# Decoder step on one core: a shared bias table row, projections between spatial-gating steps, and a pooled-row store moved ahead of the table loads

## What is computed

```python
qa,ka,va,fa,ub,vb,qc,kc,vc,pd = split(x @ w_in)
o_a = fox_attention(qa, ka, va, cumsum(log_sigmoid(fa + b)))     # A, per-head forget gate
u, v = gelu(ub), layer_norm(gelu(vb), g, b)                      # B, gating unit in chunks of 128
o_b = u * (tril(w_spatial) @ v + b_spatial)
o_c = dilated_attention(qc, kc, vc, t5_bias)                     # C, bias from a 32-bucket table
o_d = (trailing_mean(pd) - pd) @ w_pool * pool_scale             # D
x = LN(ALPHA*x + (sum_n sigmoid(x @ w_gate_n) * (o_n @ w_branch_n)) @ w_out)
x = LN(ALPHA*x + moe(x))                                         # 16 experts, top 2
```

## Time and profile before

| | us |
|---|---|
| median of 3 runs | 1513.4 |
| lowest, highest | 1512.94, 1513.81 |
| profiled execution | 1514.06 |
| its span, first to last instruction | 1512.1 |

### The profile page before, as it was taken

How to read it: one execution, slowest core, us unless ns; L and a number is a source line. 1 busy time by engine, 2 the same in 40 slices (tenths; PEclk the granted TensorE clock), 3 DMA queues, 4 the chain that set the end, 5 groups by cost and what they waited for, 6 DMA issues and landing times.

```text
span 1512.1 us, 20414 instructions
## 1 busy us (share of the span) xinstructions
PE 1371.3 (91%) x7682; PEld 1094.0 (72%) x7682; DVE 779.9 (52%) x1336; ACT 480.7 (32%) x788; POOL 322.8 (21%) x233
## 2 busy tenths in 40 slices
PE   6989989979788999999999999999928999999970
PEld 5665565756555799999999999778826666677640
DVE  3465474542245422344444344464775677777746
ACT  3311145421136311111111111221125556555636
POOL 0258910353453000000000000000245112223220
PEclk9989999999979999999999999999959999999995
DMA  7347620355601121321321431422387998887645
GB/s 226 117 134 263 212 98 1 107 182 169 221 17 32 64 81 63 108 80 64 107 80 65 144 126 66 150 78 79 122 311 280 379 310 312 297 310 254 202 153 226
DMA packets 75197, 237.72 MB, mean 157 GB/s; under 512 B 17029, under 2 KB 27476, under 8 KB 61422
## 3 DMA queue, kind: packets, MB, share of 16 engines
q1 hardware_dynamic: 48630, 160.73, 29.7%
q0 software_dynamic: 17792, 59.20, 13.2%
q10 hardware_dynamic: 8704, 16.84, 3.2%
HBM read 213.49 MB, written 65.74 MB: 185 GB/s over the span
## 4 chain that ended last, share of the span: by engine, by line
PE 83%; DMA 5%; DVE 4%; ACT 3%; issue 2%; POOL 2%; SPq 0%; DVEq 0%; POOLq 0%
PE ps L481 16%; PE ps L483 16%; PE ps L482 16%; PE ps L620 7%; PE ps L1257 6%; PE ps L1229 5%; PE ps L1253 2%; PE ps L1354 2%; PE ps L1254 2%; PE ps L1397 2%; PE ps L1255 2%; DMA b<-in_state_k 2%; PE ps L545 1%; DMA out_pool_p<-b 1%; DMA tmp_yd<-b,b 1%
## 5 line engine op out<-in xcount | busy, mean ns | idle before, releaser
L481 PE MATMUL ps<-b,b 128*128 128x344 f32 (+1 forms) x1360 | 469.1, 345 | 5.4 <-DVE b L841 2.7
L483 PE MATMUL ps<-b,b 128*128 128x344 f32 (+1 forms) x1360 | 465.1, 342 | 0.0
L482 PE MATMUL ps<-b,b 128*128 128x344 f32 (+1 forms) x1360 | 464.9, 342 | 0.0
L481 PEld LDWEIGHTS ps<-b,b 128*128 128x128 f32 x1360 | 254.9, 187 | 24.5 <-issue 3.5
L483 PEld LDWEIGHTS ps<-b,b 128*128 128x128 f32 x1360 | 254.6, 187 | 19.2 <-issue 0.9
L482 PEld LDWEIGHTS ps<-b,b 128*128 128x128 f32 x1360 | 254.6, 187 | 17.2 <-issue 0.9
L1012 DVE TENSOR_TENSOR b<-b,b 128x2048 fp32r<-128x2048 f32 x64 | 146.6, 2291 | 66.2 <-ACT b L704 60.0
L649 ACT ACTIVATE b<-ps,b 128x344 f32<-128x344 f32 x96 | 52.7, 549 | 380.2 <-PE ps L483 380.2
L1083 POOL DMA_INDIRECT tmp_xs<-b,b x36 | 43.1, 1198 | 593.1 <-issue 572.4
L1229 PE MATMUL ps<-b,b 128*128 128x128 f32 (+1 forms) x782 | 119.1, 285 | 39.2 <-DMA b<-tmp_xs 18.4
L1229 PEld LDWEIGHTS ps<-b,b 128*128 128x128 f32 (+1 forms) x782 | 93.0, 145 | 83.4 <-issue 35.6
(11 more groups left out here) (290 smaller groups left out, 1556.0 us busy)
## 6 DMA issues: line engine op xcount, KB each, us to landing
b<-in_w SPq DMA_DIRECT2D x96, 1024.0 KB
b<-in_w_merge SPq DMA_DIRECT2D x32, 640.5 KB, 4.3
tmp_xs<-b ACTq DMA_DIRECT2D x32, 514.0 KB, 4.3
b<-tmp_xs SPq DMA_DIRECT2D x32, 514.0 KB
b<-in_w_in SPq DMA_DIRECT2D x8, 1024.0 KB, 8.8
b<-in_xT SPq DMA_DIRECT2D x4, 1024.0 KB, 11.9
b<-in_w_out SPq DMA_DIRECT2D x4, 1024.0 KB, 8.2
b<-in_x SPq DMA_DIRECT2D x8, 512.0 KB, 4.0
```

The source lines that it names most:

```text
L481: mm(out, hi, mhi, start=start, stop=False)
L482: mm(out, hi, mlo, start=False, stop=False)
L483: return mm(out, lo, mhi, start=False, stop=stop)
```

## The change

1. **Bias table.** 12 matmuls with 32 output rows each, the four heads in four groups of 32 rows of the same banks (5, 6 and 7), in pieces of 512, 512 and 128 columns. ACT copies three pieces into one row block `tb_row`, and the store repeats each row four times. The PE never waits for ACT in it. DVE no longer waits for the store (`tb_out`), POOL waits for `tb_src` instead.
2. **Gating unit.** The subtraction of the mean and the gain are done per tile during the `uv` stage, the rest in one unlinked operation a tile. The `vfa` tiles, now in the order 2 to 7, 0, 1, stand between the sample tiles, the spatial matmuls and the transposes. The sample row's product comes first on DVE.
3. **Splits of the `vpd` weights** stand before the last `qkc` eviction on ACT, one weight chunk per finished chunk of the last `qkc` tile (`pk`), and earlier on DVE.
4. **Late stores.** `pool_p` is stored as soon as the last `vpd` tile is evicted, ahead of the table loads.
5. **First merged tile.** DVE makes high and low part itself: chunks 0 to 6 before the last weight's product, chunk 7 behind it. PE waits for chunk 7 only at its last k.

POOL's order of gathers and dilated keys is as before.

```diff
--- before.py
+++ after.py
...
+VFA_ORDER = (2, 3, 4, 5, 6, 7, 0, 1)
+
+PROJECTED = ([("uv", t) for t in TILE_ORDER] + [("vfa", NT)] + [("vfa", t) for t in VFA_ORDER[:2]] + [("qka", NT)]
+             + [("vfa", t) for t in VFA_ORDER[2:]]
...
-        tb_src = at(OT + 4608, [P, 4, TBW])
+        tb_row = at(PSB, [P, TBW])
...
-                pe.wait_ge(S("mlo"), s + 1)
+                pe.wait_ge(S("mlo"), s + 2 if s else 1)
+                if s == 0 and n == 0:
+                    pe.wait_ge(S("sgd"), 95)
                 if n == 0:
                     pe.wait_ge(S("wo0s"), 8)
                 for k in range(KD):
+                    if s == 0 and n == 0 and k == KD - 1:
+                        pe.wait_ge(S("mlo"), 2)
...
-            merged_high(0)
...
-            for u in range(2):
-                merge_weight(KD // 2 - 1, 3, u, u == 1)
-                split_out_weights(KD - 2 + u, KD - 1 + u)
+
+            def first_tile(chunks):
+                t = WORDER[0]
+                r = rows(t)
+                hi, m = mring[:, 0, chunks, 0:r], mT[:, chunks, t * P:t * P + r]
+                link(dve.tensor_copy(hi, m))
+                dve.tensor_tensor(mL[:, chunks, t * P:t * P + r], m, hi.bitcast(F32), ALU.subtract).then_inc(S("mlo"), 1)
+
+            merge_weight(KD // 2 - 1, 3, 0, False)
+            split_out_weights(KD - 2, KD - 1)
+            split_out_weights(KD - 1, KD)
+            first_tile(slice(0, KD - 1))
+            merge_weight(KD // 2 - 1, 3, 1, True)
             dve.sem_inc(S("merged"), 1)
+            first_tile(slice(KD - 1, KD))
...
-                dve.wait_ge(S("mhi"), s + 1)
+                dve.wait_ge(S("mhi"), s)
                 m = mT[:, :, t * P:t * P + r]
                 dve.tensor_tensor(mL[:, :, t * P:t * P + r], m, mring[:, s % 3, :, 0:r].bitcast(F32), ALU.subtract).then_inc(S("mlo"), 1)
 
-            merged_low(0)
...
-            sp.wait_ge(S("tb_src"), 12)
-            sp.dma_start(a["tb_dram"].rearrange("h (p u) -> p h u", p=P), tb_src[:]).then_inc(S("tb_out"), 16)
+            sp.wait_ge(S("tb_src"), 1)
+            sp.dma_start(a["tb_dram"].rearrange("h (r i u) -> (h r) i u", i=H, u=TBW),
+                         tb_row[:].rearrange("r (o u) -> r o u", o=1).to_broadcast([P, H, TBW])).then_inc(S("tb_out"), 16)
...
-            sp.wait_ge(S("proj"), 45)
+            sp.wait_ge(S("evicted"), pj_index("vpd", NT - 1) + 1)
+            sp.dma_start(a["pool_p"], vp[P - 15:P, NT - 1, W:2 * W]).then_inc(S("out_pool"), 16)
             for h in range(H):
                 src = a["tb_dram"][h, P - 1:P - 1 + P * (TBW - 1)].rearrange("(p u) -> p u", u=TBW - 1)[:, 0:SEQ]
                 sp.dma_start(tb[:, h, :], src).then_inc(S("tb_in"), 16)
-            sp.wait_ge(S("evicted"), pj_index("vpd", NT - 1) + 1)
             sp.dma_start(a["v_c_p"].rearrange("(t p) w -> p t w", p=P), vp[:, :, 0:W]).then_inc(S("out_vc"), 16)
-            sp.dma_start(a["pool_p"], vp[P - 15:P, NT - 1, W:2 * W]).then_inc(S("out_pool"), 16)
...
+                        if chunk == "qkc" and t == NT - 1 and k < KD - 1:
+                            m.then_inc(S("pk"), 1)
...
-            for h in range(H):
-                for q in range(3):
-                    n = h * 3 + q
-                    if n >= 2:
-                        pe.wait_ge(S("tb_src"), n - 1)
-                    mm(ps[:, 6 + n % 2, 0:384], t5[:, h:h + 1].to_broadcast([NBUCK + 1, P]), oh_rev[:, q * 384:(q + 1) * 384],
-                       start=True, stop=True).then_inc(S("tb_mm"), 1)
-            pe.wait_ge(S("tb_src"), 12)
+            for n, (lo, hi) in enumerate(TB_PARTS):
+                for h in range(H):
+                    m = mm(ps[32 * h:32 * h + 32, 5 + n, 0:hi - lo], t5[:, h:h + 1].to_broadcast([NBUCK + 1, 32]), oh_rev[:, lo:hi],
+                           start=True, stop=True)
+            m.then_inc(S("tb_mm"), 1)
             for i in range(4):
-                m = mm(ps[:, 6, i * H:(i + 1) * H], oh_dec[:, i, :], t5[:], start=True, stop=True)
+                m = mm(ps[:, 4, i * H:(i + 1) * H], oh_dec[:, i, :], t5[:], start=True, stop=True)
             m.then_inc(S("tb_mm"), 1)
 
-            project("vfa", NT)
-            project("qka", NT)
-            pe.wait_ge(S("wsp_m"), 4)
-            pe.wait_ge(S("v_done"), 1)
-            for g in range(4):
-                if g >= 2:
-                    pe.wait_ge(S("ob"), g - 1)
-                elif g == 0:
-                    pe.wait_ge(S("tb_src"), 13)
+            def spatial(g):
+                if g == 0:
+                    pe.wait_ge(S("wsp_m"), 4)
+                    pe.wait_ge(S("v_done"), 1)
+                    pe.wait_ge(S("tb_src"), 1)
+                elif g >= 2:
+                    pe.wait_ge(S("ob"), g)
                 mm(ps[:, 6 + g % 2, :].rearrange("p (t c) -> p t c", t=NT), wsp[:, g, :],
                    uv[:, 0:NT, W + 64 * g:W + 64 * g + 64], start=True, stop=True).then_inc(S("band_mm"), 1)
-            pe.wait_ge(S("ob"), 5)
-            for t in range(NT + 1):
-                if t >= 2:
-                    pe.wait_ge(S("obT"), t - 1)
-                r = rows(t)
-                for f in range(2):
-                    m = tr(ps[:, 4 + t % 2, f * P:f * P + r], uv[0:r, t, f * P:(f + 1) * P], r)
-                m.then_inc(S("ob_tr"), 1)
+
+            def ob_transposes(*tiles):
+                for t in tiles:
+                    if t == 0:
+                        pe.wait_ge(S("ob"), 5)
+                        pe.wait_ge(S("tb_src"), 2)
+                    if t >= 2:
+                        pe.wait_ge(S("obT"), t - 1)
+                    r = rows(t)
+                    for f in range(2):
+                        m = tr(ps[:, 4 + t % 2, f * P:f * P + r], uv[0:r, t, f * P:(f + 1) * P], r)
+                    m.then_inc(S("ob_tr"), 1)
+
+            project("vfa", NT)
+            project("vfa", VFA_ORDER[0])
+            project("vfa", VFA_ORDER[1])
+            project("qka", NT)
+            spatial(0)
+            spatial(1)
+            project("vfa", VFA_ORDER[2])
+            spatial(2)
+            spatial(3)
+            project("vfa", VFA_ORDER[3])
+            ob_transposes(0, 1)
+            project("vfa", VFA_ORDER[4])
+            ob_transposes(2, 3)
+            project("vfa", VFA_ORDER[5])
+            ob_transposes(4, 5)
+            project("vfa", VFA_ORDER[6])
+            ob_transposes(6, 7, 8)
+            project("vfa", VFA_ORDER[7])
...
-            for t in TILE_ORDER[1:]:
-                project("vfa", t)
...
-                if chunk == "vpd":
-                    act.wait_ge(S("proj"), pj_index("qkc", NT - 1) + 1)
                 for k in range(KD):
+                    if chunk == "vpd" and k < KD - 1:
+                        act.wait_ge(S("pk"), k + 1)
+                    elif chunk == "vpd":
+                        act.wait_ge(S("proj"), pj_index("qkc", NT - 1) + 1)
...
-            for n in range(12):
-                h, q = n // 3, n % 3
-                act.wait_ge(S("tb_mm"), n + 1)
-                act.copy(tb_src[:, h, q * 384:(q + 1) * 384], ps[:, 6 + n % 2, 0:384]).then_inc(S("tb_src"), 1)
-            act.wait_ge(S("tb_mm"), 13)
-            act.copy(bC[:].rearrange("p s h -> p (s h)"), ps[:, 6, 0:16]).then_inc(S("tb_src"), 1)
+            act.wait_ge(S("tb_mm"), 1)
+            for n, (lo, hi) in enumerate(TB_PARTS):
+                m = act.copy(tb_row[:, lo:hi], ps[:, 5 + n, 0:hi - lo])
+            m.then_inc(S("tb_src"), 1)
+            act.wait_ge(S("tb_mm"), 2)
+            act.copy(bC[:].rearrange("p s h -> p (s h)"), ps[:, 4, 0:16]).then_inc(S("tb_src"), 1)
             evict("vfa", NT)
+            evict("vfa", VFA_ORDER[0])
+            evict("vfa", VFA_ORDER[1])
             evict("qka", NT)
-            for t in TILE_ORDER[1:]:
+            for t in VFA_ORDER[2:]:
...
+                else:
+                    w_high("vpd")
                 evict("qkc", i - 1)
+                if i == 8:
+                    x_high("vpd", 1)
                 values_ready(i)
-            w_high("vpd")
-            x_high("vpd", 1)
...
+                v = uv[0:r, t, W:2 * W]
+                dve.scalar_tensor_tensor(v, v, mv[0:r, t, 0:1], gbB[0:r, 0, :], ALU.subtract, ALU.mult)
                 if 3 <= i <= 6:
                     x_low("uv", i + 1)
             dve.tensor_scalar(rs2[:], mv[:, :, 1], EPS, None, ALU.add).then_inc(S("var"), 1)
             dve.wait_ge(S("sd"), 1)
             link(dve.reciprocal(rs[:], rs[:]))
-            for t in range(NT + 1):
+            for t in range(NT, -1, -1):
                 r = rows(t)
                 v = uv[0:r, t, W:2 * W]
-                link(dve.tensor_scalar(v, v, mv[0:r, t, 0:1], rs[0:r, t:t + 1], ALU.subtract, ALU.mult))
-                link(dve.tensor_tensor(v, v, gbB[0:r, 0, :], ALU.mult))
-                link(dve.tensor_tensor(v, v, gbB[0:r, 1, :], ALU.add))
```

(22 more changed lines are left out.)

7 lines of the change are left out of this document (4 added, 3 removed).

## The result

| | us |
|---|---|
| before, median | 1513.6 |
| changed, median of 4 runs | 1494.6 |
| changed, lowest and highest | 1491.63, 1498.33 |
| changed to before | 0.9867, 95% interval 0.9833 to 0.9901 |
| span of the profiled execution | 1489.7 |

The forecast was 1496. The change took 19 us off, where the sum had 17.

What follows compares the result with a forecast made beforehand. PE, busy for 91% of 1512.1 us, was taken as the bound. Terms 0.4 + 0 - 13.3 - 4.3 = -17.2 took 1514.06 to 1496.9, less 0.7 is 1496 us; 8 in 10 range 1488 to 1503.

Steps and rivals of the forecast that it cites:

- the sum: All terms of the forecast added over the whole kernel: -17.2 us against the profiled execution of 1514.06 us.
- Late stores, -13.3: Pooling stage: `pool_p` lands early, so PE's 10.36 us of idle time and 2.9 us of slow products go.
- First merged tile, -4.3: Output projection: the idle time and low clock behind the last merge product both go, -4.3 us.
- Splits, 0: Start of `vpd`: PE's 6.98 us wait ends with a gathered decode value, so moving the splits gains 0.
- Front, +0.4: Bias table to attention A: PE gets 18 us ahead, but DVE's and ACT's lists take it away; +0.4 us.
- The eaten front: Rival, 3%: PE's stretch from 63 us to the last transposes never leaves the low clock, +29 us, 1525.
- The later front: Rival, 12%: late last transposes delay keys, logarithm and `qka` tiles, +5 to +14 us, 1501 to 1510.
- late `pool_p`: Rival, 5%: in pooling the store still lands late; only 5 to 8 of 13.3 us arrive, 1501 to 1504.
- The Trainium skill's rule: Sign against the front: transposes don't count as activity for the clock, so strewing them between `vfa` tiles could hurt.
- The passed-on front: Rival, 7%: copies or logarithm come sooner, so up to 15 of PE's 18 us at the front arrive, 1481.
- The stall of 4.82 us: Front: DVE's 480-element copy, held till POOL's product ended, should take about 0.5 us with POOL idle, 4.3 less.

Runs made afterwards that it cites:

- e6: The changed kernel with the first merged tile made as before (ACT the high part, DVE the low part, behind the last weight's product); 1498.8 us, ratio 0.9902.
- e1: The kernel before with one edit, the store of `pool_p` ahead of the table loads; 1497.9 us, ratio 0.9906.
- e2: The kernel before with one edit, DVE making the first merged tile, seven chunks ahead of the last weight's product; 1511.6 us, ratio 0.9995.
- e4: The kernel before with the `vpd` weight splits alone moved ahead of the last `qkc` eviction on ACT and earlier on DVE; 1511.5 us, ratio 0.9999.
- e3: The kernel before with the new bias table, the norms and the gating unit's new order alone; 1507.8 us, ratio 0.9972.
- e7: The changed kernel with DVE's list reordered: decode-score set-up ahead of the spatial products, key sums between copies, softplus right behind the last `vfa` tile; 1478.2 us.
- e8: The changed kernel with the eight `vfa` tiles in one block behind the transposes instead of strewn; 1487.9 us, ratio 0.9820.
- e12: The kernel before with the new bias table alone, all else as before; 1515.5 us, ratio 0.9998.
- second set: The second of three sets of follow-up runs, timed with the kernel before on the same chip; that kernel's median there was 1512.5 us (11 runs).

## Why the prediction was right, point by point

**The sum** had 17.2 us; the medians moved by 19.0 and 19.1. That it came so near is in part luck. By the runs with one edit the front was worth 4.0 us where the sum had it costing 0.4, and the first tile brought 0.2 where the sum had 4.3: two misses of some 4 us with opposite signs. By e6 the first tile brought 5.4; the parts would then add to some 23, more than the 19 measured, so the smaller figure fits the whole better, within the noise.

**Late stores, -13.3**: right, by the mechanism and the size. The landing was put at 2.1 us and was 1.4 (402.4 and 2.1 make 404.5, not the working's 404.9; nothing hangs on it). e1 gave -13.9. Both parts of the term were there, the idle time and the low clock behind it: from the second group of band products to the heads it is 5.2 us instead of 18.4, which is 13.3 less. The heads and transposes up to attention C ran 1.2 faster on top (14.9 for 16.1), which the sum had left out: their first part ran at a higher clock (0.65 over 414 to 418 us), and only then did it fall to 0.50 (418 to 422), as in the earlier trace rows.

**First merged tile, -4.3**: right at its place, 4.4 from the trace of before to that of the changed kernel. At the end it is between nothing (e2) and 5.4 (e6), so the size is not shown.

**Splits, 0**: right. e4 gave -0.3, with PE's wait unchanged.

**Front, +0.4**: the mechanism was right in each link, and the size was off by 4 us. Copies at 103.3 were 102.6, POOL's third product at 110.8 was 109.98, the end of the logarithm at 135.9 was 134.8, PE's wait of 15 us was 15.55, the last `qka` tile at 182.9 was 181.0. So the new front came within 2 us of its forecast; 0.8 of this was there at POOL's third product, the rest is a shorter stretch at the low clock behind the wait (the first tile behind it took 8.1 us instead of 9.5). What the sum had wrong is the other side of the difference: the old front was taken from one profile, in which it ran 1.7 us better than the mean of the four traces with the old front (197.40 against 199.1), with the highest clock of the four over 66 to 100 us. With both, 0.4 - 1.9 - 1.7 is -3.2; e3 measured -4.0, and the rest is within its interval.

**Rivals.** The eaten front (1525) needed a low clock in the strewn stretch; the trace shows 0.95 over 66 to 100 us. It was right to keep it small. The later front is out too, since the last `qka` tile came 1.9 earlier than forecast, and so is the late `pool_p`, which landed in 1.4 us. The Trainium skill's rule in "TensorE: Matmul & The Clock Gate", section "Part 4: PE-mode transpose", spoke against the strewn order; the trace doesn't bear it out as a cost here: groups of four to six transposes between full tiles left the clock up. The passed-on front was a real possibility, but of another kernel: e7 is 1478, close to the 1481 that it was priced at.

**The port.** The stall of 4.82 us was told from one row. e8 brought it back (4.88) by putting the copy beside POOL's product, and e12 made it 9.99 with two products. "SBUF — State Buffer" of the Trainium skill, section "SBUF: two separate sides", has it as an exclusive lock for a whole instruction, where VectorE runs in a two-port mode or reads two inputs from SBUF. The three rows agree: each held operation ends within 0.3 us of the end of POOL's. Not every operation is held, though. e7, DVE and then POOL:

```profile
89.04 2.28 DVE L1896 TENSOR_REDUCE b<-b 128x32 f32<-128x2048 f32 x1
91.30 0.76 DVE L1880 COPY b<-ps 128x256 f32<-128x256 f32 x2
```

```profile
88.83 4.59 POOL L2197 TENSOR_TENSOR b<-b,b 128x2048 f32<-128x2048 f32 x1
```

A sum of keys and two copies out of PSUM ran wholly beside POOL's product and took what they take without it (2.28 at 107.5 and 0.76 at 97.6 in the changed kernel).

## What to carry to other kernels

Look for a small store or load that somebody waits for behind large transfers on the same queue; it costs one moved line. Before shortening the work of the busiest engine, follow its first consumer through the other engines' lists: 18 us of PE were saved here and 4 arrived, and a new order of DVE's list brought 15 more. Take the base of a difference from several traces where the clock wavers.

## What the runs showed that I had not expected

- The old front's clock differs from run to run: 0.60, 0.62, 0.66 and 0.70 over 66 to 100 us, attention A's start from 197.4 to 200.8. The kernel before itself ran between 1506.6 and 1522.0 in the second set, though its first three runs had lain within 0.9 us. A few runs close together are no measure of the scatter.
- Four operations of 8 partitions and 64 elements took 9.99 us beside two products of POOL (0.97 without them), while a sum over 128 x 2048 elements beside one took its usual 2.28. What an operation costs beside POOL depends on its kind more than on its size.
- PE idle for 8.3 of 34 us and 5.5 us faster at the end (e8): in this stretch a fuller PE was the worse choice.
- The experts' stage takes 377.5 to 382.5 us from trace to trace, with or without the edits. A term of 3 us is hard to see through it.
